# Sixteen attention steps, packed modulation rows and an early start of the retention's output product in a two-block transformer kernel

## The reference, cut to what matters

```
# block 1
mod   = silu(c) @ w_ada + b_ada            # 6 x 1024 values for x; the same w_ada for the context
h, hc = rms_norm(x), rms_norm(ctx), each scaled and shifted by mod
gqa   : 8 query heads, 2 key heads of 64, keys = context 256 + tokens 256, rope, softmax
diff  : 4 heads, softmax(q1 k1) - lam * softmax(q2 k2), values of width 128
x     = x + gt1 * (concat(gqa, diff) @ w_o)
x     = x + gt2 * moe(...)                 # 32 experts, top 4, 1024 -> 2048 -> 1024
x     = rms_norm(x)
# block 2, two layers, each with its own mod = silu(c2) @ ada_w[i] + ada_b[i]
layer 0: x += g1 * ((silu(g) * group_norm(retention(q, k, v))) @ w_rout); x += g2 * conv_ffn(...)
layer 1: x += g1 * (ya * sigmoid(yb)), (ya, yb) = gelu(s5(h)) @ w_glu;    x += g2 * conv_ffn(...)
```

## Time and profile before

| | |
|---|---|
| median of 3 runs | 2389.65 us (2388.15 to 2389.77) |
| the profiled execution | 2381.07 us, of which the span of the profile is 2379.3 us |
| PE busy in the span | 2173.9 us (91%) |
| ACT, DVE, POOL busy | 422.3, 551.1, 174.5 us |
| read from memory | 625.8 MB |

### The profile page before, as it was taken

One profiled execution on the slowest core, in us unless ns is written; L12 is line 12 of the kernel. 1 busy time (PEld: TensorE's weight loads), 2 busy tenths in 40 slices (PEclk: granted clock), 3 DMA queues, 4 the chain that ended last, 5 costly groups with the idle time before them and its releaser, 6 DMA issues.

```text
span 2379.3 us, 25905 instructions
## 1 busy us (share of the span) xinstructions
PE 2173.9 (91%) x10606; PEld 1387.1 (58%) x10606; DVE 551.1 (23%) x1195; ACT 422.3 (18%) x770; POOL 174.5 (7%) x225
## 2 busy tenths in 40 slices
PE   6978868989998999899899999999999999799998
PEld 4633337444444444444444458486888888778887
DVE  1041243111111111111111124113101503610231
ACT  3112231101111111111111111112012204420111
POOL 0000000000000000000000000000064781000000
PEclk9988787999999999999999999999999999799999
DMA  9517732899999999999999993449124342434230
GB/s 364 192 68 282 257 136 76 341 399 418 418 417 408 417 418 418 418 418 418 417 408 418 418 400 122 155 169 371 65 81 146 139 148 106 177 142 142 109 122 18
DMA packets 164374, 627.88 MB, mean 264 GB/s; under 512 B 5232, under 2 KB 9456, under 8 KB 127824
## 3 DMA queue, kind: packets, MB, share of 16 engines
q1 hardware_dynamic: 163840, 625.45, 67.2%
q0 software_dynamic: 464, 1.44, 0.2%
HBM read 625.82 MB, written 1.05 MB: 263 GB/s over the span
## 4 chain that ended last, share of the span: by engine, by line
PE 74%; DMA 13%; DVE 8%; issue 2%; ACT 2%; SPq 1%; DVEq 0%; ACTq 0%
PE psum L869 31%; PE psum L1170 21%; DMA ring<-in_w_in_dram 12%; PE psum L902 3%; PE psum L880 2%; PE psum L1146 2%; PE psum L992 2%; PE psum L1190 1%; PE psum L911 1%; DVE arena L2060 1%; PE psum L1385 1%; PE psum L1058 1%; PE psum L963 1%; SPq L753 1%; DVE arena L2075 1%
## 5 line engine op out<-in xcount | busy, mean ns | idle before, releaser
L1170 PE MATMUL psum<-ring,arena 128*64 128x512 f32 x3168 | 715.5, 609 | 78.1 <-DMA ring<-in_w_in_dram 77.2
L869 PE MATMUL psum<-arena,ring 128*128 128x256 f32 (+1 forms) x3328 | 743.6, 386 | 27.2 <-ACT arena L1464 13.4
L869 PEld LDWEIGHTS psum<-arena,ring 128*128 128x128 f32 x3328 | 636.9, 192 | 131.1 <-issue 29.8
L1170 PEld LDWEIGHTS psum<-ring,arena 128*64 128x64 f32 x3168 | 240.2, 140 | 539.7 <-issue 485.2
L1583 ACT ACTIVATE arena<-psum 128x512 f32<-128x512 f32 (+1 forms) x155 | 88.5, 571 | 837.3 <-PE psum L1170 714.3
L2060 DVE TENSOR_TENSOR arena<-psum,arena 128x512 f32<-128x512 f32 (+1 forms) x68 | 44.3, 671 | 432.1 <-PE psum L1190 432.1
L1502 ACT ACTIVATE arena<-psum 128x512 f32<-128x512 f32 (+1 forms) x68 | 38.9, 573 | 385.3 <-PE psum L869 207.3
L2305 DVE SCALAR_TENSOR_TENSOR consts<-psum,smalls,consts 128x255 f32<-128x255 f32 (+1 forms) x88 | 38.4, 478 | 247.4 <-ACT consts L1714 246.7
L2047 DVE TENSOR_SCALAR arena<-consts,arena 128x64 f32<-128x64 f32 (+1 forms) x68 | 16.7, 309 | 339.0 <-PE psum L1170 339.0
L902 PE MATMUL psum<-ring,cond 128*32 128x512 f32 x576 | 86.0, 727 | 4.1 <-DMA ring<-in_w_ada_dram 3.9
L2447 POOL DMA_DIRECT2D arena<-in_pos_dram x1 | 0.6, 577 | 1038.7 <-DVE tiny L2139 1038.7
(11 more groups left out here) (336 smaller groups left out, 1600.2 us busy)
## 6 DMA issues: line engine op xcount, KB each, us to landing
ring<-in_w_in_dram SPq DMA_DIRECT2D x132, 2048.0 KB, 15.1
ring<-in_w_out_dram SPq DMA_DIRECT2D x66, 2048.0 KB, 18.0
ring<-in_w_ada_dram SPq DMA_DIRECT2D x36, 2048.0 KB, 9.4
ring<-in_w_up_dram SPq DMA_DIRECT2D x22, 2048.0 KB, 7.9
ring<-in_w_ret_dram SPq DMA_DIRECT2D x12, 2048.0 KB, 12.9
ring<-in_w_down_dram SPq DMA_DIRECT2D x16, 1408.0 KB, 5.7
ring<-in_w_qkv_dram SPq DMA_DIRECT2D x4, 2048.0 KB, 19.0
ring<-in_w_rout_dram SPq DMA_DIRECT2D x4, 2048.0 KB, 10.4
```

What stands on the lines that cost most here:

```text
L869: ins = nc.tensor.matmul(bank(c)[:, at:at + n], w[:, k, m * P:m * P + P], r, start=(k == 0), stop=(k == k_tiles - 1))
L1170: ins = nc.tensor.matmul(psum[at:at + CAP, p, :], act[:, k, CAP * e:CAP * e + CAP], w[:, kk, n0:n0 + BANK], start=(k < 3 - halves), stop=( ...
```

## The change

Four things are changed.

1. **Modulation packed by four slabs.** The condition stands in a wider buffer of zeros (`cond32` 38 wide, `cond32_2` 35 wide), and slab s of a group takes a window shifted by s, so that the rows of four slabs accumulate in one bank (`ROWS_BANK`, outside the chunks in number) at different partitions. One copy by ACT and four matmuls against a `pick` of 8 columns (before 128) then serve four slabs. There are 9 groups. A slab's slot is free once its rows are made (`rows_used`).
2. **Sixteen attention steps.** Every step takes two maps: for the grouped heads the two halves (partitions 0 and 64) of one tile. PE's order in a step is: both scores of the next step, the turns of this one, columns of a group that has ended, one or two slabs of rows (`STEP_SLABS`), and in odd steps the values. In the attention, chunks use banks 2 and 3 only. Head-norm sums leave the chunk rotation (banks 4 to 6), and the ropes move forward, none after the last value tile; the first scores wait for eight ropes.
3. **Retention.** `rout` slab 0 starts (12 of its 16 tiles) ahead of `rvar` of the last head, slab 1 behind it, in banks 6 and 7; the last four tiles of both follow when the last head is done.
4. **S5 and glu.** DVE finishes `from_frame` of all parts ahead of the gelu, and copies odd lags one part late; ACT squares the next part ahead of the lag copies; PE takes the first three chunks of `glu` part by part, as gelu parts are written, then the fourth chunk.

```
-ROPES_AFTER = [(2, 3), (5, 6), (7, 8), (0, 1, 4)]
+ROPES_AFTER = [(2, 3), (5, 6, 7), (8, 0, 4, 1), ()]
+STEPS = 16
+STEP_SLABS = [2, 1, 1, 1] * 4
+ROWS_BANK = [4, 0, 1, 0, 1, 0, 4, 5, 4]
...
-    steps = [("rs", 0), "ada2"]
+    steps = ["ada2", ("rs", 0), "ada2"]
     for h in range(RET_HEADS):
         steps += [("ro", h, 0), ("ro", h, 1), "ada2", ("rmean", h)]
         if h < RET_HEADS - 1:
             steps += [("rs", h + 1)]
-        steps += ["ada2", ("rvar", h)]
         if h < RET_HEADS - 1:
-            steps += ["ada2"]
+            steps += ["ada2", ("rvar", h), "ada2"]
+        else:
+            steps += [("rout", 0), ("rvar", h), ("rout", 1)]
...
+                group, s = MOD_NUMBER[key] // 4, MOD_NUMBER[key] % 4
...
+                    at = cond32[:, k, 6 - 2 * s:38 - 2 * s] if key[0] == "ada" else cond32_2[:, k, 3 - s:35 - s]
+                    ins = nc.tensor.matmul(psum[32 * q:32 * q + 32, b, :], at, w[:, k, :],
+                                           start=(s == 0 and k < 4), stop=(s == 3 and k >= 4))
+                ins.then_inc(rows_used, 1)
...
+                for m in range(4):
+                    ins = nc.tensor.matmul(bank(key)[:, 8 * m:8 * m + 8], rows_of(group)[:, m * P:m * P + P],
+                                           con("pick"), start=True, stop=True)
...
+            for t in range(STEPS):
+                if t + 1 < STEPS:
+                    scores(t + 1)
+                for n, maps in turns_of(t):
+                    turn(n, maps)
+                for group in ended:
+                    modulation_cols(group)
+                for key in ATT_SLABS[t]:
+                    modulation_rows(key)
+                ended = groups_ending(ATT_SLABS[t])
+                if t % 2 and t < 8:
+                    values_a(t // 2)
+                elif t % 2:
+                    values_b((t - 8) // 2)
...
+            for t in range(STEPS):
+                copy_values(t)
+                for a in range(2):
+                    if t + 1 < STEPS:
+                        probabilities(2 * t + 2 + a)
+                    if a < len(turns_of(t)):
+                        copy_turned(t, a)
+                for group in groups_ending(ATT_SLABS[t]):
+                    copy_rows(group)
...
+                if kind == "rout":
+                    pe.wait_ge(ret_done, RET_HEADS - 1)
+                    arrived(step)
+                    rout_tiles(h, 0, 12)
+                    continue
...
+            for part in range(S5_PARTS):
+                pe.wait_ge(s5_y_even, part + 1)
+                pe.wait_ge(s5_y_odd, part + 1)
+                glu_part([(("glu", 0), 0), (("glu", 0), 1), (("glu", 1), 0)], part)
+            for part in range(S5_PARTS):
+                glu_part([(("glu", 1), 1)], part)
...
+            gelu_square(0)
+            for part in range(S5_PARTS):
+                act.wait_ge(s5_gelu_in, part + 1)
+                nc.scalar.activation(y_of(part), y_of(part), ACT.Tanh, scale=GELU_C).then_inc(s5_gelu_t, 1)
+                if part + 1 < S5_PARTS:
+                    gelu_square(part + 1)
+                even_lags(part)
```

More of the change, by code:

```diff
@@ L174, in plan, with take_turns @@
 def plan():
-    chunks, slabs = {}, {}
+    chunks, slabs, bank, use = {}, {}, {}, {}
+    uses = [0] * 4
+    turn = {"among": (0, 1, 2, 3), "next": 0}
+    def take_turns(*banks):
+        turn.update(among=banks, next=0)
     def chunk(*keys):
@@ L182, in chunk @@
             chunks[k] = len(chunks)
+            b = turn["among"][turn["next"] % len(turn["among"])]
+            bank[k], use[k] = b, uses[b]
+            uses[b] += 1
+            turn["next"] += 1
     def slab(key, n):
@@ L187, in slab @@
         slabs[key] = len(chunks)
-    def modulation(keys, first=None, flush=True):
-        for i, key in enumerate(keys):
-            slab(key, 1)
-            before = keys[i - 1] if i else first
-            if before:
-                chunk(("cols", before))
-        if flush:
-            chunk(("cols", keys[-1]))
     chunk(("norm", 1), ("norm", 0))
-    modulation([("ada", s) for s in range(4)])
+    for key in MOD_KEYS[:4]:
+        slab(key, 0)
+    chunk(("cols", 0))
     slab("qa", 2)
@@ L204, in plan @@
     slab("kb", 4)
-    chunk(*(("qknorm", i) for i in range(3)))
     for t in range(KEY_TILES):
@@ L263, in plan @@
     chunk(("norm", 8))
[L264 to L267 removed]
+    return chunks, bank, use, slabs, rope_uses, before_loop
+CHUNK, BANK_OF, USE, SLABS, ROPE_USES, SLABS_1 = plan()
 SLAB_KEYS = list(SLABS)
@@ L382, in transformer_blocks_kernel @@
         rows = rope_t
+        turned = [p_t[:, n, :].rearrange("p (k t) -> p k t", t=T) for n in range(2)]
+        turned += [h_all[:, 4 * n:4 * n + 4, T:N_KEYS] for n in range(2)]
         mix = h_all[:, :, 0:T]
@@ L1048, in _, with values_a @@
-            modulation_cols(before)
+            def values_a(i):
+                key = ("oa", i)
+                begin(key)
+                pe.wait_ge(pt_ready, 4 * i + 4)
+                if i == 0:
+                    copied(pe, ("kva", 1))
+                for kt in range(KEY_TILES):
+                    for a in range(2):
+                        ins = nc.tensor.matmul(half(key, 0)[a * HD:a * HD + HD], v_all[:, kt, a * HD:a * HD + HD],
+                                               turned_at(2 * i, a)[:, kt, :],
+                                               start=(kt == 0), stop=(kt == KEY_TILES - 1))
+                end(ins)
@@ new lines, in values_b @@
+            def values_b(j):
+                key = ("ob", j)
+                begin(key)
+                pe.wait_ge(pt_ready, 18 + 2 * j)
+                if j == 0:
+                    for i in range(4):
+                        copied(pe, ("vb", i))
+                for kt in range(KEY_TILES):
+                    ins = nc.tensor.matmul(half(key, 0), v_all[:, kt, P * (j + 1):P * (j + 1) + P],
+                                           turned_at(8 + 2 * j, 0)[:, kt, :],
+                                           start=(kt == 0), stop=(kt == KEY_TILES - 1))
+                end(ins)
@@ L1401, in _, with glu_part @@
                 chunk_outputs(part)
-            pe.wait_ge(s5_y_even, S5_PARTS)
-            pe.wait_ge(s5_y_odd, S5_PARTS)
-            for s in range(4):
+            def glu_part(keys, part):
+                for key in keys:
+                    (_, s), c = key
+                    if part == 0:
+                        begin(key)
+                    for k in (2 * part, 2 * part + 1):
+                        for m in range(2):
+                            at = P * (2 * c + m)
+                            ins = nc.tensor.matmul(half(key, m), slab(("glu", s))[:, k, at:at + P], y5[:, k, :],
+                                                   start=(k == 0 and m == 0), stop=(k == KD - 1 and m == 1))
+                    if part == S5_PARTS - 1:
+                        end(ins)
+            arrived(("glu", 0))
+            arrived(("glu", 1))
+            for part in range(S5_PARTS):
[4 more added lines that the diff above has]
+                glu_part([(("glu", 1), 1)], part)
+            for s in range(2, 4):
                 features(("glu", s), lambda k: y5[:, k, :], 2)
@@ L1656, in _ @@
                 if kind == "ada2":
-                    copy_rows(step)
+                    for group in groups_ending([step]):
+                        copy_rows(group)
                 elif kind == "ro":
```

433 lines of the change are left out of this document (209 added, 224 removed).

## The result

The changed kernel takes 2251.37 us (median of 4 runs, 2250.14 to 2255.6) against 2388.9 us for the kernel before in the runs beside it: ratio 0.9434, interval 0.942 to 0.9448. I had predicted 2273, so the medians are 137.5 us apart rather than 116, and the time lies 1.4 us above the lower end of the range (2250 to 2302). Some 8 us of the 137.5 belong to the median of the kernel before, which was lower in every later group of runs (2383.35 to 2384.57): the two profiled executions, 2381.07 and 2251.53 us, are 129.5 us apart. The span of the profile is 2249.7 us, before 2379.3.

What follows compares the result with a forecast made beforehand. Attention was taken as bound by hand-overs between three engines, the expert loop by weights, the retention as dense PE work. Gains 9.7 + 77.7 + 15.1 + 13.5 = 116.0 from 2389.65 gave 2273.6, forecast 2273 us, range 2250 to 2302.

Steps and rivals of the forecast that it cites:

- the six rivals: Clock stays low, ACT's copies bind, slow slabs, new waits (0.05), slower than before (0.02), attention unchanged (0.03).
- the early gain: Ahead of the expert loop: time gained there survives, since the loop starts from a full ring and still costs 987 us.
- term B: Attention, first scores to output product: 103.9 us against 181.6, a gain of 77.7 us.
- Term A: Start of the attention: first scores at 147.0 rather than 156.66, gain 9.7 us, bounds 8.4 to 10.5.
- my bound of 85: Attention: upper bound of the gain, 85 us, with no waits and no clock loss.
- S + 5.0: Odd grouped attention step: values wait for the second copy until 5.0 us after S, the start of its pair of scores.
- the hold of 4.35: Attention step: the next pair of scores can't start before 4.35 us after the start of this one.
- Rival 1: Attention: the clock stays at 0.80, PE's 92 us of work become 115, whole 2292; chance 0.15 together with rival 2.
- rival 2: Attention: each step waits for both turned copies by ACT, 19 us go, whole 2292; chance 0.15 together with Rival 1.
- Rival 3: Attention: slabs come at 282 GB/s, 7.4 us each, so it ends 11 us later, whole 2284; chance 0.07.
- Term C: Retention with its output product: 117.0 us against 132.14, gain 15.1, with 0.4 us to spare before new waits.
- Term D: S5 and glu: glu ends at 2112.7 rather than 2126.2, gain 13.5 us, bounds 10 to 18.

Runs made afterwards that it cites:

- after_again: The changed kernel run once more as it is: 2252.89 us, ratio 0.9451 against the kernel before.
- values_by_head: The changed kernel with the grouped heads' values made one head after the other, as in the old order: 2256.3 us, ratio 0.9462.
- before_values_by_tile: The kernel before with only the two loops of the grouped heads' values exchanged, so that the heads take turns: 2376.03 us, ratio 0.9973.
- after: The changed kernel in its first profiled run: 2251.53 us profiled, median 2251.37 us, ratio 0.9434 against the kernel before.
- ropes_as_before: The changed kernel with the ropes in their old places and the first scores waiting for all nine: 2260.54 us, ratio 0.9481.
- columns_four_times: The changed kernel with each group's four column matmuls issued four times over, still 8 columns wide: 2292.77 us, ratio 0.9615.
- turns_first: The changed kernel with each attention step's turns put ahead of the next step's scores again: 2267.25 us, ratio 0.951.
- rout_late: The changed kernel with both slabs of the retention's output product begun only when the last head is done: 2264.24 us, ratio 0.9496.
- glu_whole: The changed kernel with the glu product waiting for all four gelu parts before it starts: 2267.09 us, ratio 0.9508.

## Why the prediction was right or wrong

**Mechanisms.** The four terms came in the places and of the kinds that were forecast, and none of the six rivals did. But the time isn't in the band that I gave 0.66 (2258 to 2281). It is where I had put 0.02, for no waits, full clock and no offset from the profiled run. It got there partly for another reason: the clock was full and there was no offset, but the waits stayed, and the faster value products, which I hadn't thought of, made up for them. That the time still lies in the range is luck in that part. The loop shows the DMA share at 1.01 and 413 GB/s, so the early gain wasn't lent. The profiled execution was forecast at 2265 and took 2251.5: 13.5 us, of which 11.0 are term B, 4.5 the loop, and -2.1 the terms A and D. The other 8.6 us between 2273.6 and 2251.5 are the offset that I carried over.

**Term A**, forecast 9.7, measured 8.4 here and 9.5 in after_again; the wait of 0.6 us for the second early rope is there (0.66). The missing 1.3 us stand ahead of the part that I worked out: value tile 2 starts at 122.80 where I had 121.6, and at 121.67 in after_again. Right.

**Term B**, forecast 77.7 (103.9 us), measured 88.7 (92.86), past my bound of 85. Its parts, from the starts of the score products:

| | forecast | measured |
|---|---|---|
| first gap | 3.8 | 3.85 (148.29 to 152.14) |
| eight grouped steps without columns | 52.2 | 44.6 (152.14 to 198.35, less 2 x 0.8) |
| eight differential steps without columns | 40.9 | 40.4 (198.35 to 241.15, less 3 x 0.8) |
| columns of five groups | 3.5 | 4.0 |
| half clock | 3.5 | 0 |

The step of the prediction that failed most is "values 2.8 for grouped heads": I took the duration from the earlier trace rows as if the product were untouched, and the diff had exchanged the two loops inside it. values_by_head and before_values_by_tile show 0.9 us per product, 3.7 for the four. I also had an odd step's values wait for the second copy until S + 5.0; they start at S + 4.6 (157.80 to 162.39), and in one step, where columns stand ahead of them, without a wait: 2.2 over four steps. Even steps take 5.66 with two slabs (157.80 - 152.14) and 4.06 with one (168.33 - 164.27), where I had 6.1 and 4.4: the hold of 4.35 that I had put on the next scores didn't bind in the grouped half. It binds once in the differential half, at 4.06 rather than 4.35 (209.78 to 213.84, with a wait of 0.49). That is 1.7 over four steps, and 3.7 + 2.2 + 1.7 is the 7.6. The rest of the 11.0 is nearly all the half clock, which I had put at 3.5 and which cost nothing. The bound of 85 was no bound because it kept the 2.8: it was passed by 3.7, the four value products.

**The clock** was the weakest term: I had scaled it from short gaps of the kernel before. The gap of 2.72 us, longer than those of the earlier trace rows, was followed by full clock in five traces, after and after_again among them, and by half clock in three: values_by_head (rows at 4.84), ropes_as_before (where a gap of 4.41 stands before it) and columns_four_times (scores at 2.08 in both). So one gap of that size can go either way, and the 3.5 us that I allowed were neither confirmed nor refuted by the change's own trace: that they cost nothing there is in part luck. With repeated gaps, as in turns_first, the mean is 0.95. Rival 1 (clock stays 0.80) is refuted; rival 2 too: PE waits for ACT's copies 0.6 us in three of the steps, some 2 us rather than 19. Rival 3 failed on the rate: 370 GB/s, and no wait for a slab in the attention. (My own sum for the weights was off: 147 + 15 x 5.1 is 223.5, not 228; SP had issued the fifteenth slab by 221.1.)

**Term C**, forecast 117.0 us, measured 116.88, no wait; the 0.4 us to spare held. The size was right, and rout_late shows that its reason was thinner than I wrote: with the cover gone, 13.1 us go, not the 4.55 of the visible wait. The price of missing cover includes the half clock behind it.

**Term D**, forecast 13.5, measured 12.7 and 15.1. From the first product of `glu` to its end I had 60.0 us (2052.7 to 2112.7); it is 59.9 (1936.66 to 1996.57). The wait at the third chunk is there, 2.50.

**Columns.** The Trainium skill's figure (TensorE: Matmul & The Clock Gate, LDWEIGHTS) gave an estimated 0.85 us for eight loads, against 0.97 from the row. In after the next start follows a group by 0.80 to 0.81 in two places (240.34 to 241.15, 1577.36 to 1578.16), though the record is 0.95 long. Elsewhere it is 0.88 to 0.89, but there the product ahead gives some 0.1 back: the turns at 169.39 are followed after 0.93 (at 170.32) by columns, where turns without columns behind them are followed after 1.02. Here the page was nearer than my row, by about 1 us over the nine groups, since I used a record's length where the distance of starts counts.

**The loop and the offset.** I carried over 8.6 us by which the median before lay above its profiled run. It should not have been carried: the kernel before ran from 2376.05 to 2389.77 over four groups of runs, and after's median (2251.37) equals its profiled run (2251.53). The chain of waits shows one source. Passes of the loop in after, the second of them long:

```profile
382.40 19.37 DMA ring<-in_w_in_dram
401.91 7.09 PE psum L1215 x32
...
442.59 19.43 DMA ring<-in_w_in_dram
462.15 8.40 PE psum L1215 x32
...
504.12 18.28 DMA ring<-in_w_in_dram
522.54 7.09 PE psum L1215 x32
...
685.00 18.12 DMA ring<-in_w_in_dram
703.26 7.09 PE psum L1215 x32
```

The last 32 products of a pass stand behind a wait for a slab and take 7.09 us, or more when the clock falls there: 10.0 us in three passes before, 8.4 in two of after (462.15, 643.01), 10.0 in two of after_again. Those sum to 8.9, 2.6 and 5.9 us over the ordinary, but the loop doesn't pay all of it, since the next wait for a slab is shorter (18.28 and 18.12 in place of 19.4). What a long pass costs is the distance to the next: an ordinary one is 60.24 us (401.91 to 462.15), one with 8.4 at most 60.39 (462.15 to 522.54), one with 10.0 61.5 to 62.1. That makes 4.3 us before, 0.2 in after and 3.4 in after_again, and the loops (1012.61, 1008.15, 1011.74) differ by nearly as much. So the 4.5 us are not shown to be the change's: the loop takes 1009.63 us in values_by_head, 1011.11 in turns_first and 1012.96 in glu_whole, whose edits don't touch it, and 1011.20 in before_values_by_tile.

## What to carry to other kernels

When a duration is taken from the trace for an operation that "stays", compare the loop order inside it in the diff: two products of 64 output partitions that alternate took 1.95 us, in sequence 2.83. Price idle time of the PE with the half clock that may stand behind it, and place work that needs nothing (weights' rows, an output product's ready tiles) directly in front of each hand-over: 12.6 us came back from two waits of 8.6. Don't carry the difference between a median and one traced run over to another kernel before several runs have shown what it is.

## What the runs showed of the hardware

- **Half clock behind narrow products, with no idle engine.** 32 records of 8 columns moved took 3.64 us, and the slab's rows behind them 2.79 instead of 1.92 with no bracket between; with 128 columns moved the group took 3.74 and the rows 1.92. The mean granted clock of the attention was 0.93 against 1.00. Widening these products, whose time goes with the number of weight loads, made the kernel 15.7 us faster, some 10 of them in or behind such groups. Why the chip grants less there is not settled by these runs.
- **The same gap, another clock.** Behind the 2.72 us gap at the start of the attention five traces went on at full clock and three at half; behind the waits of about 2.9 us in the loop most passes went on at full clock, and one to three of 16 did not in each of the twelve traces. A single trace doesn't price such a gap.
- **Two loops exchanged, seen in two kernels.** Alternating between two outputs of 64 partitions is worth 0.9 us for 16 records, in either kernel (2.83 to 1.95, 2.86 to 1.95).
- **In a stretch bound by loads, a slow piece is partly absorbed.** 3 us more in the last products of a pass lengthened the pass by 1.3 to 1.8, and 1.3 us more by at most 0.15, since the wait for the next slab got shorter.
